# Second layer of a two-layer decoder: decay exponentials one strip later, the first strips' copies between the weight splits, the recurrence's third chunk first and ahead of the last memory values

## The reference, cut to what matters

```python
def rwkv7_time_mix(proj, mu, w0, w2, a0, a2, g2, k_k, k_a, r_k, ln_g, ln_b):
    xs = proj + (prev - proj) * mu                      # prev: proj shifted by one token
    r, k, v, wl, al, gl = jnp.split(xs, offs, axis=-1)
    w = -jax.nn.softplus(-(w0 + jnp.tanh(wl) @ w2)) - 0.5
    decay = jnp.exp(-jnp.exp(w))
    a = jax.nn.sigmoid(a0 + al @ a2)
    g = jax.nn.sigmoid(gl) @ g2
    kk = (k * k_k); kk = kk * lax.rsqrt(jnp.maximum(jnp.sum(kk * kk, axis=-1, keepdims=True), 1e-24))
    k = k * (1.0 + (a - 1.0) * k_a)
    def step(state, inp):
        r_t, w_t, k_t, v_t, a_t, b_t = inp              # a_t = -kk, b_t = kk * a
        sa = jnp.einsum('bhij,bhj->bhi', state, a_t)
        state = state * w_t[:, :, None, :] + sa[..., None] * b_t[:, :, None, :] + v_t[..., None] * k_t[:, :, None, :]
        return state, jnp.einsum('bhij,bhj->bhi', state, r_t)
    ...
    bonus = jnp.sum(rh * kh * r_k, axis=-1, keepdims=True) * vh
    return (normalised y + bonus) * g

# reference(), layer 1
proj = hn @ rwkv_w_in[j]
prim = rwkv7_time_mix(proj[..., :RWKV_SHIFT_W], ...)
mo = memory_attention(proj[..., -MEM_WIDTH:], mem_k, mem_v)   # softmax(q k^T / 8) v per head
h = h + rmsnorm(jnp.concatenate([prim, mo], -1) @ w_out[i], post_mix_g[i])
```

## Time and profile before

| | us |
|---|---|
| Median of three executions | 743.8 (742.77 to 743.83) |
| Profiled execution, its own time | 743.27 |
| Span of the profiled execution | 741.5 |
| PE busy | 704.7 (95%) |
| DVE busy | 471.0 (64%) |
| ACT busy | 415.9 (56%) |
| POOL busy | 118.1 (16%) |
| Granted TensorE clock, mean | 0.999 of full speed |

### The profile page before, as it was taken

One profiled execution on the slowest core, in us unless ns is written; L12 is line 12 of the kernel. 1 busy time (PEld: TensorE's weight loads), 2 busy tenths in 40 slices (PEclk: granted clock), 3 DMA queues, 4 the chain that ended last, 5 costly groups with the idle time before them and its releaser, 6 DMA issues.

```text
span 741.5 us, 14711 instructions
## 1 busy us (share of the span) xinstructions
PE 704.7 (95%) x6287; PEld 610.5 (82%) x6287; DVE 471.0 (64%) x664; ACT 415.9 (56%) x674; POOL 118.1 (16%) x163
## 2 busy tenths in 40 slices
PE   4999989999999999999999998999899999999996
PEld 3789965788888888888889887988688888888885
DVE  3778788747865765544666878544668765666423
ACT  5753868647665465532898745543268565465311
POOL 8111067700000000000350076600000000000000
PEclk9999999999999999999999999999999999999999
DMA  8946820008665565454755340000057566556511
GB/s 301 328 130 200 302 67 2 1 1 281 204 200 196 171 196 201 174 204 133 237 175 171 115 154 20 4 5 4 1 184 243 171 192 205 170 188 210 172 55 57
DMA packets 78275, 111.68 MB, mean 151 GB/s; under 512 B 2124, under 2 KB 64738, under 8 KB 78210
## 3 DMA queue, kind: packets, MB, share of 16 engines
q1 hardware_dynamic: 77090, 107.67, 43.6%
q0 software_dynamic: 976, 3.04, 1.3%
q10 hardware_dynamic: 144, 0.04, 0.0%
HBM read 109.68 MB, written 1.05 MB: 149 GB/s over the span
## 4 chain that ended last, share of the span: by engine, by line
PE 82%; DVE 7%; ACT 7%; issue 2%; DMA 1%; DVEq 0%; SPq 0%; ACTq 0%
PE ps L1040 20%; PE ps L737 12%; PE ps L738 12%; PE ps L739 12%; PE ps L1043 10%; PE ps L1216 6%; ACT w_hi L1417 3%; PE ps L1226 2%; DVE w_lo L1882 2%; PE ps L895 1%; DMA hn<-mem 1%; PE ps L869 1%; PE ps L844 1%; PE ps L818 1%; PE ps L1234 1%
## 5 line engine op out<-in xcount | busy, mean ns | idle before, releaser
L1882 DVE TENSOR_TENSOR w_lo<-w_raw,w_hi 128x2048 fp32r<-128x2048 f32 (+2 forms) x101 | 227.7, 2268 | 103.4 <-ACT w_hi L1417 103.3
L1417 ACT ACTIVATE w_hi<-w_raw 128x2048 fp32r<-128x2048 f32 (+2 forms) x101 | 189.1, 1892 | 48.6 <-PE ps L739 41.8
L1040 PE MATMUL ps<-x_hi_lo,w_hi 128*128 128x512 f32 x640 | 201.2, 396 | 0.0
L1043 PEld LDWEIGHTS ps<-x_hi_lo,w_lo 128*128 128x128 f32 x640 | 120.2, 188 | 28.4
L1043 PE MATMUL ps<-x_hi_lo,w_lo 128*128 128x256 f32 x640 | 125.7, 278 | 0.0
L1040 PEld LDWEIGHTS ps<-x_hi_lo,w_hi 128*128 128x128 f32 x640 | 97.4, 189 | 0.0
L737 PE MATMUL ps<-w_hi,x_hi_lo 128*128 128x512 f32 (+3 forms) x240 | 83.1, 346 | 5.8 <-DVE x_hi_lo L2102 4.4
L738 PE MATMUL ps<-w_lo,x_hi_lo 128*128 128x512 f32 (+3 forms) x240 | 81.0, 338 | 0.0
L739 PE MATMUL ps<-w_hi,x_hi_lo 128*128 128x512 f32 (+3 forms) x240 | 81.0, 337 | 0.0
L737 PE MATMUL ps<-w_hi,hidden_hi 128*128 128x512 f32 x176 | 68.6, 390 | 0.0
L738 PE MATMUL ps<-w_lo,hidden_hi 128*128 128x512 f32 x176 | 68.5, 389 | 0.0
(11 more groups left out here) (367 smaller groups left out, 1067.1 us busy)
## 6 DMA issues: line engine op xcount, KB each, us to landing
w_raw<-w_ffn_in SPq DMA_DIRECT2D x44, 1024.0 KB, 5.1
w_raw<-w_ffn_out SPq DMA_DIRECT2D x22, 1024.0 KB, 4.9
w_raw<-rwkv_w_in SPq DMA_DIRECT2D x11, 1024.0 KB, 5.4
w_raw<-w_out SPq DMA_DIRECT2D x8, 1024.0 KB, 5.0
w_raw<-nsa_w_in SPq DMA_DIRECT2D x6, 1024.0 KB, 14.4
w_raw<-w_mem_kv SPq DMA_DIRECT2D x2, 1024.0 KB, 9.3
w_raw<-nsa_cmp_k_w SPq DMA_DIRECT2D x2, 1024.0 KB, 5.5
w_raw<-nsa_cmp_v_w SPq DMA_DIRECT2D x2, 1024.0 KB, 5.5
```

The source lines that it names most:

```text
L1040: pe.matmul(psum[:, bank + j, :], kt_of(w_hi, i, k)[:, cols[j]], xx[:, k, :, :].rearrange("p c n -> p (c n)"), start=k == 0, stop=False)
L1043: ins = pe.matmul(psum[:, bank + j, 0:SEQ], kt_of(w_lo, i, k)[:, cols[j]], xh[:, k, :], start=False, stop=k == KD - 1)
L1417: act.activation(w_hi[:, i % SPL, 0:size(i)], raw[:, i % RAW, 0:size(i)], ACT.Copy).then_inc(hi_done, 1)
L1882: dve.tensor_tensor(w_lo[:, i % RAW, 0:size(i)], raw[:, i % RAW, 0:size(i)], w_hi[:, i % SPL, 0:size(i)], ALU.subtract).then_inc(lo_done, 1)
```

## The change

Four parts:

1. ACT, start of layer 1: of the three splits at the end of the join, which stood ahead of the four `strip_tok` copies, two now stand behind the first two copies and one behind the last two.
2. ACT, strip loop: `eP` and `eN` move from q = 5 to q = 6, behind `strip_out(6)`.
3. PE: the cross products of chunk 2 (`rates(EARLY)`) stand between `memory_step(6)` and `memory_step(7)`, without a wait for `bo_ev`; chunks 0, 1 and 3 follow behind step 7 with waits for 2, 3 and 3 of the bonus products.
4. PE, ACT, DVE, POOL: the loops over the chunks, from the masks to the inverse, run in the order 2, 0, 1, 3 in place of 0, 1, 2, 3.

```diff
+        EARLY, *LATER = CHUNKS = (2, 0, 1, 3)
@@ POOL
-            for c in range(NCH):
+            for c in CHUNKS:
                 pool.wait_ge(pv[c], step(DVE_STEPS, "Dt"))
@@ PE
             memory_step(6)
-            memory_step(7)
...
+            def rates(c):
+                cross((c, 0), rows64(aC, c), ar(c, 0), FEAT, TOK)
+                cross((c, 1), ar(c, 0), rows64(aC, c), FEAT, TOK).then_inc(pm[c], 1)
+
             pe.wait_ge(fm_out, MQ + 4)
-            pe.wait_ge(bo_ev, 3)
             pe.wait_ge(ar_ok, 2)
             pe.wait_ge(bk_ok, 1)
             pe.wait_ge(shifted, 10)
             pe.wait_ge(rwkv_ok, 7)
-            for c in range(NCH):
+            rates(EARLY)
+            memory_step(7)
+            for c in LATER:
+                pe.wait_ge(bo_ev, min(c + 2, 3))
                 if c == NCH - 1:
                     pe.wait_ge(a_lo, N_UNITS - NMEM + 1)
-                cross((c, 0), rows64(aC, c), ar(c, 0), FEAT, TOK)
-                cross((c, 1), ar(c, 0), rows64(aC, c), FEAT, TOK).then_inc(pm[c], 1)
-            for c in range(NCH):
+                rates(c)
+            for c in CHUNKS:
                 V(c, "D")
...
@@ ACT
+            def tok_out(t):
+                for q in range(2):
+                    if t == 0:
+                        act.wait_ge(f_mm, 2 + q + 1)
+                    else:
+                        act.wait_ge(used, first["rwkv"] + q + 1)
+                    act.activation(tm[:, t, q, :], psum[:, turn_bank(1, t) + q, 0:FC], ACT.Copy).then_inc(f_ev, 1)
+
             def join(m, last_piece):
...
                     tile_hi(m, t)
+                if m == 1:
+                    for t in range(TT):
+                        tok_out(t)
+                        split_to(last_piece + 4 + t)
                 split_to(last_piece + 5)
...
-            for t in range(TT):
-                tok_out(t)
             for q in range(11):
...
                     act.activation(eP_sq[:], eP_sq[:], ACT.Exp, scale=-0.5).then_inc(ss_rt, 1)
+                if q == 6:
                     act.wait_ge(cs_ok, 1)
                     act.activation(eP[:], cs[:], ACT.Exp, scale=-KAPPA).then_inc(ex_ok, 1)
...
```

More of the change, by code:

```diff
@@ L1686, in _ @@
             join(1, first["down", 0] + N_DOWN)
-            def tok_out(t):
-                for q in range(2):
-                    if t == 0:
-                        act.wait_ge(f_mm, 2 + q + 1)
-                    else:
-                        act.wait_ge(used, first["rwkv"] + q + 1)
-                    act.activation(tm[:, t, q, :], psum[:, turn_bank(1, t) + q, 0:FC], ACT.Copy).then_inc(f_ev, 1)
             def strip_out(q):
```

## The result

| | before | after |
|---|---|---|
| Median of six executions each, same chip, us | 743.77 (741.09 to 745.08) | 738.38 (736.41 to 740.68) |
| Profiled execution, us | 743.27 | 736.41 |
| Its span, us | 741.5 | 734.7 |
| PE busy, us | 704.7 (95%) | 705.1 (96%) |

The ratio is 0.9927, with a 95% interval of 0.9908 to 0.9947, so the change gives 5.4 us (3.9 to 6.8). The forecast was 739.9 with a range from 738.4 to 742.1; the median is 0.02 under its low end, and the gain is near that of rival B (738.7).

The account below looks back on a forecast made before the run. PE, busy 95% of the span, was taken as the bound, so only its idle time could be gained. 0.5 + 1.5 + 1.9 = 3.9 us off the 743.8 median gave 739.9 us, range 738.4 to 742.1.

Parts of the forecast that it names:

- rival B: Crosses and squarings on PE: supply gaps vanish, since PE waits among crosses while instructions arrive; 5.1 us, 738.7; chance 0.11.
- Part 1, 0.5 forecast: PE at strip 0's turn and second lora_pairs: 0.5 of 1.65 us of waits survives as gain, the rest only moves.
- grown bracket: PE's idle wait before the second lora_pairs, 0.60 us before, forecast near 1.1 after the change.
- Part 2, 1.5 forecast: PE before strip 8: the 1.49 us wait for strip 6's copies goes altogether, readers of the exponentials still covered; 1.5 us.
- rival C: Softmax: exponentials or DVE's maxima, covered by about 0.1 us only, come late and give part 2 back; 741.3; chance 0.07.
- Part 3, 1.9 forecast: PE's crosses to squarings: unbroken squarings from 451.3 instead of 455.28, 3.98 less the 2.0 already gained, so 1.9 us.
- upper bound: Crosses to squarings: 3.1 us if no supply gaps remain and DVE's masks bound the squarings; 5.1 in all.
- both gaps that the forecast had kept: PE among crosses and first squarings: "issue" gaps near 1 us, next blocks supplied only at 447.6 and 451.3.
- the page's answer, 5.1: Instruction supply on PE: blocks of 256 fetched ahead, cost mostly hidden, so the whole change would give 5.1 us.
- Part 4, nothing forecast: Chunk order on PE, ACT, DVE, POOL: worth nothing by itself, only lets chunk 2's masks be first.
- A: PE's crosses and squarings: instruction supply isn't helped; only 2.0 to 3.2 us gained, about 741.2; chance 0.18.
- D: POOL's multiplications, stretched by moved DVE work, make PE 6.4 us later; net 2.5 slower, 746.3; chance 0.03.

Follow-up runs that it names:

- part 1: Kernel before with only the strip_tok copies moved between the splits on ACT: 742.78 us, ratio 0.9995.
- parts 1 and 2: Kernel before with only ACT's edits, the copies between the splits and the exponentials one strip later: 741.45 us, ratio 0.9973.
- held kernel: Changed kernel with one more PE wait, for the first bonus product (bo_ev at least 1), ahead of chunk 2's crosses: 739.16 us, ratio 0.9957.
- padded changed kernel: Changed kernel with 36 extra 64x8 products, results unused, ahead of strip 8 to move the block edges: 746.49 us, ratio 1.005.
- padded kernel before: Kernel before with 16 extra 64x8 products, results unused, ahead of strip 8 to move the block edges: 742.99 us, ratio 1.0003.

## Why the prediction fell short, step by step

**Part 1, 0.5 forecast.** The trace has 0.56 at its place, and the grown bracket, forecast near 1.1, is 1.30. The turn of strip 0 no longer waits. The chain of reasons held: the third split in front of `strip_out(0)`, DVE's low part ahead of `shift(0)`, ACT's tanh behind that.

**Part 2, 1.5 forecast.** It gave 1.73. The bracket of 1.49 before strip 8 went as a whole, the exponentials' reader was covered, and rival C fell. The 0.2 more is in how a bracket is read (last section). Together the two parts were worth 2.3 in the trace and 2.0 in the medians of their own experiment.

**Part 3, 1.9 forecast: the term that was mis-sized.** It gave 2.9 to 3.2 in its own trace and 3.0 (5.27 - 2.29) in the change's, close to the 3.1 which the prediction gave as its upper bound, "with no supply gaps at all". The step that failed stands in two sentences: "some 27 records on, at 446.7, the supplied block ends. It began 4 records into chunk 2's crosses, at 444.25; with 3.3 the next comes at 447.6." The place of the block edge was about right. What was wrong is the clock that I started there. In the kernel before, PE's start of the crosses and the end of a wait are the same moment, 448.26, so 3.3 us "from the start of the block" and 3.3 us "from the end of the wait" could not be told apart in the rows, and I took the first. The experiments speak for the second. Where a wait holds PE at the edge, the packet comes 0.94 to 0.95 behind its end (449.21 and 448.26 before, the same in part 1 and in parts 1 and 2; 445.04 and 444.09 in the held kernel), with the padded changed kernel as the exception (0.15). Where none stands there, it comes ahead of PE's arrival (442.01 and 442.34 in the change; in the padded kernel before, whose edge lies 32 records further up the list, at 441.53, 7.7 ahead of the crosses). So no 3.3 us ran from PE's first cross: the next block was there when PE needed it, and both gaps that the forecast had kept, near 446.7 and 450.3, stayed away. The change takes the wait for the bonus from the edge and puts it a cross and the values further on, so the block is under way while PE still turns probabilities. That the instruction fetch is driven by PE's sequencer, which runs ahead of the multiplications until a wait stops it, is my reading of these times; the trace has no row for a request, and the exception shows that it is not the whole of it.

The Trainium skill, page "Runtime: NRT & Kernel Launch", section "Instruction fetch mechanics", says that the sequencer fetches the next block while the current one is worked off and that the cost is mostly hidden. In the changed kernel the trace agrees, with no gap around 442 to 450 us. In the kernel before it does not, with 1.25 and 0.82 us, nor in the held one, with 0.95 and 1.19. The prediction set the page's answer, 5.1, beside its own and went by the rows; the measured 5.4 is the page's side.

**Part 4, nothing forecast.** Nothing was found in the trace.

**The sum.** 0.5 + 1.5 + 1.9 = 3.9 was forecast (the 1.9 is 3.98 - 2.0, so rather 2.0), 0.56 + 1.73 + 3.0 = 5.3 measured in the trace and 5.4 in the medians. Of the missing 1.4, 1.1 is part 3.

**The rivals.** B ("the supply gaps vanish") is what happened, with a reason other than the one given, "because PE now waits among the crosses while instructions arrive": PE is held among the crosses for some 0.2 us only, at 445.36, and that is behind the start of the second block (444.85), which had come in time. "Against it: two blocks still hold almost nothing but crosses" was no objection, since the first of them was asked for before the burst began. A and C are excluded by part 3's 2.9 and by the missing bracket before strip 8. D did not occur: POOL's rows are the same to 0.01 us. Of what was to show the forecast, the "issue" gaps near 1 us are absent, and a wait that was not forecast is there, 0.37 behind the masks; DVE's masks are the bound that the prediction used for its upper end. None of the signs that it named for being wrong appeared.

## What to carry to other kernels

An "issue" gap in a dense burst of small instructions is a question of when its block was asked for. Look whether a semaphore wait stands near the block's start, and move the wait behind work that PE can already do; look for the block's packet, and count from that, not from PE's first instruction. When a gap has two possible clocks that coincide in the one trace at hand, forecast both and keep both in the range. A wait taken away from one instruction by moving a split or a copy is a loan: here 0.72 us gained at one place was paid back with 1.2 us at two others, 25 and 37 us on.

## What the runs showed of the hardware

**A bracket is less than what a stop costs.** Rows of the kernel before, around the bracket of 1.49 before strip 8:

```profile
417.11 0.28 PE L738 MATMUL ps<-x_hi_lo,w_hi 128*128 128x256 f32 x1
417.23 0.28 PE L739 MATMUL ps<-x_hi_lo,w_lo 128*128 128x256 f32 x1
...
419.20 0.28 PE L738 MATMUL ps<-x_hi_lo,w_hi 128*128 128x256 f32 x1
```

Products start every 0.12 us, so the next was due at 417.35, but the bracket counts from the modelled end, 417.51. And the first product behind the stop (419.00) is followed after 0.20 instead of 0.12. So the stop costs 419.00 - 417.35 + 0.08 = 1.73, just what part 2 gave. Likewise 1.21 was gained at the turn of strip 0, whose bracket was 1.05.

**PE's clock fell at tiny products and behind them.** The 36 extra products are 72 records. The first 42 start 58 ns apart, the last 30 some 107 ns. The busy time by stretch of that kernel (the number behind the POOL column is the granted clock):

```profile
417.60:420.00 2.40, 2.40 (x42) 2.40 (x42) 2.25 (x4) 2.40 (x3) 0.00 (x0) 1.00 0.50 84
420.00:425.00 5.00, 5.00 (x41) 4.97 (x40) 1.56 (x5) 1.19 (x1) 0.00 (x0) 0.50 0.42 173
...
426.00:428.00 2.00, 2.00 (x16) 1.87 (x15) 0.00 (x0) 0.00 (x0) 0.00 (x0) 0.79 0.00 0
428.00:430.00 2.00, 2.00 (x16) 1.67 (x16) 1.26 (x4) 0.36 (x1) 0.00 (x0) 1.00 0.00 0
```

The clock was at 2.4 GHz, fell to 1.2 GHz at 420, while PE was doing nothing but 64x8 products on 64 rows, and stayed there until about 426.8, the second half of which was ordinary work behind them. That is why they cost 7.5 us. The sixteen products did the same on a smaller scale: they ran at the full clock themselves, but 1.0 us behind the last of them, in strip 8's ordinary products, the clock fell to 1.2 GHz and stayed there from 419.5 to 422.8. That is 1.5 of their 1.92. No other kernel here, with none of these products, has a stretch at 1.2 GHz between 300 and 520 us. PE counts as 100% busy all the while.

**The squarings run close to the supply.** A block of 128 squaring records takes 128 x 28.8 ns = 3.7 us of PE, and behind a packet that took over 1.35 us the next begins only 4.0 us later in the median. It may be a part of the 1 to 2 us by which executions of one kernel differ; these runs don't settle that.
